# Thirteen modulation chunks of a diffusion step taken from TensorE to VectorE, ScalarE and GpSimd

## What is computed

```python
mod = silu(cond) @ ada_w + ada_b          # cond: 2 rows (context, latent); ada_w (2048, 9 * 2048)
sh1, sc1, g1, sh2, sc2, g2, sh3, sc3, g3 = split(mod, 9)
x = x + 0.5 * g1 * swiglu(modulate(rms_norm(x), sh1, sc1), wi1, wo1)    # FFN 1, D_FF = 5632
x = x + g2 * mixer(modulate(rms_norm(x), sh2, sc2))                     # mLSTM and attention
x = x + 0.5 * g3 * swiglu(modulate(rms_norm(x), sh3, sc3), wi2, wo2)    # FFN 2
```

## Time and profile before

| | |
|---|---|
| median of 3 runs | 2316.37 us (2316.35 to 2316.68) |
| the profiled execution | 2317.81 us, its span 2316.0 us |
| PE matmul busy | 2276.8 us, 98% |
| DVE, ACT, POOL busy | 1248.7, 934.2, 64.0 us |
| mean granted TensorE clock | 0.998 |
| DMA | 548 MB, mean 237 GB/s |

### The profile page before, as it was taken

One profiled execution on the slowest core, in us unless ns is written; L12 is line 12 of the kernel. 1 busy time (PEld: TensorE's weight loads), 2 busy tenths in 40 slices (PEclk: granted clock), 3 DMA queues, 4 the chain that ended last, 5 costly groups with the idle time before them and its releaser, 6 DMA issues.

```text
span 2316.0 us, 28893 instructions
## 1 busy us (share of the span) xinstructions
PE 2276.8 (98%) x11107; PEld 1783.3 (77%) x11107; DVE 1248.7 (54%) x1316; ACT 934.2 (40%) x1096; POOL 64.0 (3%) x55
## 2 busy tenths in 40 slices
PE   6999999999999999999999999999999999999998
PEld 3567777777777777778888888887788888888887
DVE  3445544554455548444866454555455555555557
ACT  3233333333333335344554444454344434444442
POOL 0010000000000000000510000100000000000000
PEclk9999999999999999999999999999999999999999
DMA  9998877778787876873544665748875555555553
GB/s 357 382 369 290 290 277 278 282 268 298 259 301 248 308 259 213 309 245 119 186 155 129 199 199 183 254 162 302 285 231 182 191 189 196 185 197 182 198 183 126
DMA packets 273194, 548.04 MB, mean 237 GB/s; under 512 B 9022, under 2 KB 9190, under 8 KB 272880
## 3 DMA queue, kind: packets, MB, share of 16 engines
q1 hardware_dynamic: 212388, 421.59, 53.3%
q10 hardware_dynamic: 57724, 115.92, 13.9%
q0 software_dynamic: 3024, 9.71, 1.5%
HBM read 543.73 MB, written 3.46 MB: 236 GB/s over the span
## 4 chain that ended last, share of the span: by engine, by line
PE 94%; DVE 3%; DMA 2%; ACT 1%; issue 0%; SPq 0%; DVEq 0%; ACTq 0%
PE ps L602 28%; PE ps L604 28%; PE ps L603 28%; PE ps L543 5%; DMA ada_w_sb<-in_ada_w 2%; PE ps L705 1%; DVE w_lo L1588 1%; PE ps L578 1%; PE ps L556 1%; PE ps L589 0%; PE ps L960 0%; PE ps L1028 0%; PE ps L1036 0%; ACT w_hi L1197 0%; PE ps L563 0%
## 5 line engine op out<-in xcount | busy, mean ns | idle before, releaser
L1588 DVE TENSOR_TENSOR w_lo<-raw_w,w_hi 128x1024 fp32r<-128x1024 f32 x728 | 896.6, 1234 | 856.7 <-ACT w_hi L1197 855.6
L1197 ACT CAST w_hi<-raw_w 128x1024 fp32r<-128x1024 f32 x728 | 764.5, 1052 | 1222.7 <-PE ps L604 1172.0
L602 PE MATMUL ps<-w_hi,xT_hi 128*128 128x512 f32 x2080 | 825.9, 397 | 6.1 <-DVE xT_lo L1637 3.3
L604 PE MATMUL ps<-w_hi,xT_lo 128*128 128x512 f32 x2080 | 811.3, 390 | 0.0
L603 PE MATMUL ps<-w_lo,xT_hi 128*128 128x512 f32 x2080 | 810.7, 390 | 0.0
L602 PEld LDWEIGHTS ps<-w_hi,xT_hi 128*128 128x128 f32 x2080 | 390.9, 188 | 122.0 <-issue 35.4
L604 PEld LDWEIGHTS ps<-w_hi,xT_lo 128*128 128x128 f32 x2080 | 390.9, 188 | 83.2
L603 PEld LDWEIGHTS ps<-w_lo,xT_hi 128*128 128x128 f32 x2080 | 391.3, 188 | 77.5
L602 PE MATMUL ps<-w_hi,hT_hi 128*128 128x512 f32 x704 | 275.7, 392 | 2.8 <-DVE hT_lo L1706 2.8
L603 PE MATMUL ps<-w_lo,hT_hi 128*128 128x512 f32 x704 | 274.1, 389 | 0.0
L604 PE MATMUL ps<-w_hi,hT_lo 128*128 128x512 f32 x704 | 274.0, 389 | 0.0
(11 more groups left out here) (257 smaller groups left out, 868.5 us busy)
## 6 DMA issues: line engine op xcount, KB each, us to landing
raw_w<-in_ffn_wi SPq DMA_DIRECT2D x176, 1024.0 KB, 5.1
ada_w_sb<-in_ada_w ACTq DMA_DIRECT2D x108, 1024.0 KB, 10.4
raw_w<-in_ffn_wo SPq DMA_DIRECT2D x88, 1024.0 KB, 5.2
raw_w<-in_w_in SPq DMA_DIRECT2D x68, 1024.0 KB, 5.2
ada_w_sb<-in_ada_w SPq DMA_DIRECT2D x34, 1024.0 KB, 12.2
raw_w<-in_w_out SPq DMA_DIRECT2D x16, 1024.0 KB, 5.2
raw_w<-in_w_proj_m SPq DMA_DIRECT2D x8, 1024.0 KB, 5.2
raw_w<-in_w_proj_a SPq DMA_DIRECT2D x8, 1024.0 KB, 5.2
```

The lines of the kernel that those rows point to most:

```text
L602: pe.matmul(out, a_hi, w_hi[:, slot, kk, :], start=(first and kk == 0), stop=False)
L604: mm = pe.matmul(out, a_lo, w_hi[:, slot, kk, :], start=False, stop=(last and kk == 1))
L1197: act.copy(w_hi[:, us % SPL, :, :], raw_w[:, slot, 2 * half:2 * half + 2, :]).then_inc(hi_ready, 1)
L1588: dve.tensor_tensor(w_lo[:, us % SPL, :, :], raw_w[:, slot, 2 * half:2 * half + 2, :], w_hi[:, us % SPL, :, :].bitcast(F32), ALU.subtract) ...
```

## The change

Thirteen chunks are no longer multiplied by PE: the second chunk of each of the nine loop iterations of FFN 1 (the odd chunks 11 to 27), and the four of G3. For such a chunk each of the 16 blocks of 128 weight rows (a 128 by 512 piece) is multiplied on its own:

- DVE, for the context row: `products` multiplies block k with the partition's scalar and adds it to `vec_acc[:, CTX]` (one `tensor_scalar`, then 15 `scalar_tensor_tensor`);
- ACT, for the latent row: `products` writes block k times its scalar to one of two halves of `vec_tmp`; product k waits for POOL's add k-2;
- POOL: `vec_sums` adds these to `vec_acc[:, LAT]`, 15 adds a chunk.

`MACS` says at which of the 24 units each k stands. Then PE sums over the partitions with four matmuls by a column of ones (`vec_sum`), which waits for all 16 products of DVE and all 15 adds. In FFN 1 it stands after unit 21, in FFN 2 after unit 17. The G3 chunks move to FFN 2's iterations 2 to 5, one in each, and that loop is cut in two. In the prologue two tiles of chunks 5 and 7 also go to `ada_x`, so that POOL's memset of `acc` comes after chunk 7. POOL's first gate store and load stand behind 135 adds, and the load waits for the last products.

```diff
+VEC0 = FCH - 2
+MACS = ({9: (0, 1), 10: (2, 3), 11: (4, 5), 12: (6, 7), 13: (8, 9), 14: (10,), 16: (11, 12), 18: (13, 14), 20: (15,)},
+        {5: (0,), 6: (1, 2), 7: (3,), 8: (4, 5), 9: (6, 7), 10: (8, 9), 11: (10,), 12: (11,), 13: (12, 13), 14: (14,), 16: (15,)})
...
+        vec_acc = place("vec_acc", [P, GROUPS, CH], at=SLOT + 32768)
+        vec_tmp = place("vec_tmp", [P, 2, CH], at=MN)
...
-                    if n == 3 and q < 2:
+                    if n in (3, 5, 7) and q < 2:
+                        at_least(sp, ada_used, 4 * n + q - 7 if n > 3 else 0)
                         sp.dma_start(ada_x[:, q, :, :], w[:, :, c * CH:(c + 1) * CH]).then_inc(ada_x_landed[q], 16)
...
-            pool.wait_ge(ada_used, 4 * 4)
+            pool.wait_ge(ada_used, 4 * 8)
             pool.memset(acc[:], 0.0).then_inc(acc_done, 1)
...
+            def vec_sums(n):
+                for k in range(1, KD):
+                    pool.wait_ge(prod_done, KD * n + k + 1)
+                    if k == 1:
+                        first = vec_tmp[:, 0, :]
+                    else:
+                        first = vec_acc[:, LAT, :]
+                        pool.wait_ge(mac_pool, (KD - 1) * n + k - 1)
+                    pool.tensor_tensor(vec_acc[:, LAT, :], first, vec_tmp[:, k % 2, :], ALU.add).then_inc(mac_pool, 1)
+
+            for n in range(VEC0):
+                vec_sums(n)
             pool.wait_ge(gate_rows_ready, FCH - 2)
             gate_store(0, 0)
             pool.wait_ge(gate_stored, 16)
-            pool.wait_ge(ada_used, 4 * (ADA_PRE + 2 * (FCH - 1)))
+            pool.wait_ge(mac_dve, KD * VEC0)
+            pool.wait_ge(prod_done, KD * VEC0)
             gate_load(0)
...
+            def vec_sum(c, n):
+                pe.wait_ge(ada_rows_done, c)
+                pe.wait_ge(mac_dve, KD * (n + 1))
+                pe.wait_ge(mac_pool, (KD - 1) * (n + 1))
+                flat = ctile[:].rearrange("p k c -> p (k c)")
+                for j in range(4):
+                    o = (16, 15, 18, 18)[j]
+                    mm = pe.matmul(ps[32 * j:32 * j + 32, 6, :], flat[:, o:o + 32], vec_acc[:, j % 2, :], start=True, stop=True)
+                mm.then_inc(ada_used, 4)
...
                             ada_T(ada)
-                            ada_acc(ada + 1)
...
+            def products(at, c, n, v):
+                for k in MACS[at].get(v, ()):
+                    q, j = k // 4, k % 4
+                    if j == 0:
+                        act.wait_ge(ada_landed[q], landed(c, q))
+                    if k == 0:
+                        act.wait_ge(ada_used, 4 * c)
+                    if k > 1:
+                        act.wait_ge(mac_pool, n * (KD - 1) + max(1, k - 2))
+                    act.activation(vec_tmp[:, k % 2, :], ada_w_sb[:, q, j, :], ACT.Copy,
+                                   scale=ctile[:, k, LAT:LAT + 1]).then_inc(prod_done, 1)
...
+                def products(at, c, n, v):
+                    for k in MACS[at].get(v, ()):
+                        q, j = k // 4, k % 4
+                        if j == 0:
+                            dve.wait_ge(ada_landed[q], landed(c, q))
+                        scale = ctile[:, k, CTX:CTX + 1]
+                        if k == 0:
+                            ins = dve.tensor_scalar(vec_acc[:, CTX, :], ada_w_sb[:, q, j, :], scale, None, ALU.mult)
+                        else:
+                            dve.wait_ge(mac_dve, n * KD + k)
+                            ins = dve.scalar_tensor_tensor(vec_acc[:, CTX, :], ada_w_sb[:, q, j, :], scale, vec_acc[:, CTX, :],
+                                                           ALU.mult, ALU.add)
+                        ins.then_inc(mac_dve, 1)
```

More of the change, by code:

```diff
@@ L306, in landed @@
         def landed(c, q):
-            return 16 * (c + 1) - (16 if q < 2 and (not isinstance(c, int) or c > 3) else 0)
+            if q > 1:
+                return 16 * (c + 1)
+            return 16 * (c + 1 - min(3, (c - 1) // 2 if c > 1 else 0)) if isinstance(c, int) else 16 * (c - 2)
         def at_least(eng, s, v):
@@ L769, in g_between @@
                             h_transposes(0)
[L770 to L782, removed]
@@ L784, in ffn, with step @@
                     x_chunk(u0 + 16, 0, 0, g_between)
                     pe.wait_ge(h_done, FCH + 1)
-                    x_chunk(u0 + 24, 0, 2, u_between)
-                    ffn_out(0, u0 + 32, 0, between=out_between)
+                    x_chunk(u0 + 24, 0, 2)
+                    ffn_out(0, u0 + 32, 0)
                     h_transposes(1)
[L789 to L792, removed]
+                def step(i, between=None, a=None):
+                    ffn_in(i, u0 + 16, (i - 1) * 24, a)
+                    ffn_out(i - 1, u0 + 32, (i - 1) * 24, between=between)
+                    if a is not None:
@@ L793, in ffn, with between @@
                         pe.wait_ge(gate_rows_ready, i - 1)
-                        ada_sel(2 * i + ADA_PRE - 1)
+                        ada_sel(a + 1)
                     h_transposes(i)
+                if f == 0:
+                    with pe.Fori(2, FCH) as i:
+                        def between(n):
+                            if n == 2:
+                                vec_sum(2 * i + ADA_PRE - 1, i - 2)
+                        step(i, between, 2 * i + ADA_PRE - 2)
+                else:
+                    with pe.Fori(2, 6) as i:
+                        c = i + 4 * G3 - 2
+                        def between(n):
+                            if n == 0:
+                                vec_sum(c, i + VEC0 - 2)
+                            if n == 1:
+                                ada_sel(c)
+                            if n == 2:
+                                ada_T(c)
+                        step(i, between)
+                    pe.wait_ge(ada_cols_done, 4 * NMOD)
+                    gate_T((G3,))
+                    with pe.Fori(6, FCH) as i:
+                        step(i)
@@ L1318, in step @@
                         split(u0 + 32 + k + AHEAD, ux)
-                        if f == 0 and k == 1:
-                            ada_load(2 * i + ADA_PRE, 0, range(2) if last else range(4))
+                        if f == 0 and not (isinstance(i, int) and i == 1):
+                            products(0, 2 * i + ADA_PRE - 1, i - 2, 16 + k)
+                        if g3:
+                            products(1, i + 4 * G3 - 2, i + VEC0 - 2, 16 + k)
+                        if f == 0 and k in (2, 5) and not last:
+                            ada_load(2 * i + ADA_PRE, 0, (2 + k // 5,), (i - 2) * KD)
                 def prologue():
```

121 lines of the change are left out of this document (61 added, 60 removed).

## The result

| | changed kernel |
|---|---|
| median of 4 runs | 2410.64 us (2405.71 to 2412.89) |
| before, on the same chip | 2316.52 us (2316.35 to 2316.74) |
| ratio | 1.0403, 95% interval 1.0385 to 1.0421 |
| the profiled execution | 2409.69 us, its span 2407.7 us |
| mean granted TensorE clock | 0.987 |

The forecast was 2440 us in a range of 2380 to 2505. The loss is +94 us where I had +124.

A forecast was written before the change was run, and what follows sets the result against it. The prediction took PE, busy for 98% of the span, as the bound. Its terms -0.6 + 79 + 28 + 4 + 13 summed to +123, from 2316.4 to 2440 us, in a range of 2380 to 2505.

The forecast's parts named there:

- The mechanism: A DVE instruction with two SBUF inputs and a POOL one exclude each other for their whole length, making PE late.
- The second rival: Only DVE's splits are held by POOL's adds, its products aren't: 2336 us, slower; chance 0.10.
- the first: Rival: POOL's adds don't hold DVE's work, so PE is never late: 2290 us, faster; chance 0.07.
- The third rival: POOL's add has a fixed part, 1.4 us each, with a full clock price: 2500 us; chance 0.10.
- DVE's stretch in FFN 1: DVE busy or held 47.5 us from unit 9, 18 by POOL; iterations 84.0 against 75.2 us, +79 us over nine.
- my lower bound: Some three of 15 adds fall beside h, acc and small copies (-47) and the clock costs nothing (-13): 2380 us.
- The clock: PE about half busy around units 15 to 18, so the granted clock likely falls: 1 us an iteration, +13 us.
- FFN 2: Iterations 2 to 5 take 77.4 against 66.2 us, +45; chunks leaving the first two give back 17: +28 us.
- The gate: End of FFN 1: its load waits for DVE's last product and arrives 4.9 us later than wanted: +4 us.
- The prologue: More room for chunks 5 and 7 can end PE's wait of 0.62 us: -0.6 us.
- The point from which the adds decide: Whether adds hold DVE decides the outcome from where they cost it about 0.6 us each.
- The slack of 5.7 us: A split stands ready some 2.5 us after its unit began and is needed at 8.2, three units on.

The follow-up runs named there:

- e1: The changed kernel with POOL's first add of a chunk a memset and the others on 8 of 512 columns, all waits kept; 2286.8 us.
- e3: The changed kernel with DVE's fifteen multiply-and-adds a chunk on 8 of 512 columns, ACT's products and POOL's adds kept; 2290.4 us.
- e6: The changed kernel with FFN 2's blocks started one unit earlier, one a unit over units 4 to 17 (two in units 9 and 12); 2414.0 us.
- e4: The changed kernel without POOL's adds and ACT's products: DVE makes both rows, PE takes four blocks a chunk in FFN 1; 2297.4 us.
- e7: As e4, with the twelve blocks of an FFN 1 iteration in units 8 to 19 in place of 9 to 20; 2291.7 us.
- e5: The changed kernel with POOL's first add of a chunk a memset and the others on 256 of 512 columns; 2288.8 us.
- e8: The changed kernel with POOL's first add of a chunk a memset and the others on 384 of 512 columns; 2346.9 us.

## Why the prediction was right, and what was mis-sized

**The mechanism** was right in its place, kind and direction: e1 takes the adds' reading away and leaves the rest, and 124 us go with it. That products are held like splits, which rested on no row, is shown by e3. The second rival is out with it, and the first is what e1 shows when the hold is absent: 2287 us for its 2290. The third rival, an add with a fixed part, is half true: the shortest record grows by 283 ns from 384 to 512 columns (1016 to 1299), so some 0.17 us of it don't go by columns. But DVE doesn't pay for them: it is held for 1.1 us at most.

**DVE's stretch in FFN 1.** Predicted from its split during unit 9 to the last product: 47.5 - 1.3 = 46.2 us. Measured 445.11 - 401.18 = 43.9. The term that was too large is "15 x 1.2 = 18 us": it is 14.9, or 1.0 us an add. A held split takes 2.31 - 1.22 = 1.1 us more, a held product 1670 - 747 = 0.9 us in the medians of the change and of e1. My 1.2 was half of a 1024-column POOL record; half of what the split lost beside it, 3.43 - 1.22 = 2.2 us, would have given 1.1. That adds would fall beside h or `acc`, as my lower bound had it, hardly happened: one of 195 began there. Of PE's part outside this stretch I had 37.8 us and it is 82.2 - 43.9 = 38.3. Without the clock 84.0 came out as 81.9 (below): 19 of the 32 us by which the total was too high (+123.4 for +91.7 in the profiled spans). "Products at a mean near 1.8" was a sign too far: the mean is 1380 ns, since of the 14.9 us a chunk the products take (1380 - 748) x 15 ns = 9.5 and the splits 5.4.

**The clock** fell as feared, and cost little. Windows of the change (clock after the POOL column):

```profile
415.00:420.00 5.00, 4.38 (x21) 3.21 (x19) 4.96 (x3) 2.75 (x4) 4.57 (x4) 1.00 0.81 282
420.00:425.00 5.00, 2.64 (x11) 2.00 (x9) 4.96 (x5) 3.24 (x4) 2.77 (x2) 0.88 0.92 326
425.00:430.00 5.00, 4.93 (x17) 3.60 (x16) 5.00 (x4) 1.09 (x2) 2.20 (x2) 0.77 0.48 144
```

It falls behind the 2.36 us in which PE stood still, while DVE goes on at its own pace and sets the end. e6, whose FFN 1 is that of the change, gives the price: its first two loop iterations have no fall and take 81.9 us. One fall of 3.4 us, as in seven iterations of the change, makes it 82.2; a second, behind the stop at `vec_sum`, makes it 83.8, in two of them. That is 9 x 0.3 + 2 x 1.6 = +6 us in FFN 1, where I had 9. In FFN 2, where I had 4, it can't be told from the rest.

**FFN 2.** Iterations of 76.3 us, the clock in them, for my 77.4 without it, so +40 for +45 and 4; the chunks gone from the first two iterations gave 18 us (e4's same stretches against those of before), where I had 17. Together +22 for +28 and the clock's 4.

**The gate**, +4 us. Timeline of DVE at the end of FFN 1:

```profile
956.14 1.22 DVE L1843 TENSOR_TENSOR acc<-acc,gate_bc 128x1024 f32<-128x1024 f32 x1 [4.55 <-DMA gate_bc<-gate_dram]
```

It waits 4.55 us for the landing, and from FFN 1's last transposes to FFN 2's first the change takes 734.6 us and e4 729.6. The six experiments in which POOL's work stands ahead of the gate, e1 with no hold among them, all wait for the landing (e1 4.04 us, e6 3.23) and take 731.9 to 733.6; e4 and e7 don't wait. So the later gate is shown and its price is 2 to 5 us; whether it is late by the adds or by DVE's last product, the runs don't tell apart.

**The prologue**, -0.6: it cannot be told. The first transposes come 1.2 us earlier than before, but in the eight experiments they lie between 159.6 and 162.0 us. PE's waits for the chunks' tiles didn't go: 12.4 us over the run, from 10.4.

**The point from which the adds decide.** I had said 0.6 us each. The runs give about 5.3 / 15 = 0.35: at 5.1 us of hold a chunk (e5) nothing is late in FFN 1, at 10.0 (e8) 4.7 us. The slack of 5.7 us that I had derived for a split is near the 5.3 measured. No run shows that it is the same thing: in e8 PE waits for splits for 13.8 us over the run, but for `vec_sum`'s last product 20.3 and for h 12.2.

## What to carry to other kernels

Before moving work to GpSimd, look at what VectorE does beside it: if GpSimd's instruction reads SBUF and VectorE's have two SBUF inputs, the two engines are nearly one for that time, however idle each looks in the totals. Giving VectorE the whole of it, but for four of 16 blocks in FFN 1 that went back to TensorE, was 119 us faster than sharing it (e7). Compare the holds with the slack of the engine's deadlines: here 5.3 us an FFN 1 iteration was free and what lay above was paid nearly in full. And ask where TensorE will stand still in one piece: an iteration with the same stretch on VectorE took 2 us more where the clock's fall came behind everything else (e6).

## What the runs showed of the hardware that I had not expected

- A GpSimd add of 8 columns holds VectorE up by nothing that shows (product 748 ns, against 744 with no GpSimd at all in e4), though its shortest record is 515 ns. The shortest records were 515, 735, 1016 and 1299 ns at 8, 256, 384 and 512 columns, and the longest hold of a split 0, 0.54, 0.82 and 1.10 us: it goes by the columns, 2.1 ns each, and is shorter than the record at each size. On the average of a chunk's adds (14 in e1, e5 and e8, where the first is a memset) it was about 0, 0.36, 0.71 and, of 15, 1.0 us.
- The hold doesn't depend on the size of the VectorE instruction that waits: 8 columns waited 0.9 us (1139 - 211 ns).
- A GpSimd memset of 512 columns took 0.53 us, and 390 of them beside VectorE's products left its means unchanged (748 and 1234 ns).
